# Modulation by quarters and drive chunks begun inside the modulation phase

## What is computed

```python
cond = silu(c)
mod = cond @ w_ada + b_ada                    # 2048 -> 6 * 2048
shift1, scale1, gate1, shift2, scale2, gate2 = split(mod, 6)
h = rms(x, norm1_w) * (1 + scale1) + shift1
proj = h @ w_in                               # 2048 -> 4096
u, q, k, v = split(proj, 4)                   # 1024 columns each
y_ssm = s5_mixer(u, a, dt, b, c, d, w_glu)    # a complex state space model
y_att = dilated_attention(q, k, v)
x = x + gate1 * (concat(y_ssm, y_att) @ w_out)
```

## Time and profile before

| | us |
|---|---|
| median of 3 runs | 3235.0 (3232.37 to 3236.44) |
| the profiled execution | 3236.82 |
| its span | 3234.4 |
| PE busy | 3163.7 (98%) |
| DVE busy | 1813.1 (56%) |
| ACT busy | 1243.5 (38%) |
| POOL busy | 153.2 (5%) |

### The profile page before, as it was taken

The page is one execution under the profiler, slowest core; times in us unless marked ns, Lnnn a source line. Parts: engine busy times, 40 slices in busy tenths (PEclk is TensorE's granted clock), DMA queues, the critical chain, the costliest instruction groups (busy, mean ns, idle before and its releaser), DMA issues.

```text
span 3234.4 us, 56009 instructions
## 1 busy us (share of the span) xinstructions
PE 3163.7 (98%) x24596; PEld 3029.4 (94%) x24596; DVE 1813.1 (56%) x1689; ACT 1243.5 (38%) x1192; POOL 153.2 (5%) x182
## 2 busy tenths in 40 slices
PE   6799999999999999999999999999999999999999
PEld 3599979999999999999999999999999998998997
DVE  0699876775455455654544544555556544454454
ACT  2376633433333333433333333343334333333333
POOL 1534100000000000000000000000030000000000
PEclk7799999999999999999999999999999999999999
DMA  9876667776555555555555555567535555555554
GB/s 346 293 251 235 231 230 247 249 264 222 183 182 182 182 182 182 182 170 179 171 175 175 171 180 170 180 174 152 130 124 186 180 192 180 187 182 190 186 182 156
DMA packets 329090, 631.92 MB, mean 195 GB/s; under 512 B 22452, under 2 KB 24264, under 8 KB 328664
## 3 DMA queue, kind: packets, MB, share of 16 engines
q1 hardware_dynamic: 317896, 626.16, 59.7%
q10 hardware_dynamic: 11040, 3.51, 0.5%
HBM read 627.53 MB, written 2.10 MB: 195 GB/s over the span
## 4 chain that ended last, share of the span: by engine, by line
PE 81%; DVE 3%; issue 1%; ACT 1%; DMA 0%; DVEq 0%; ACTq 0%
PE ps L579 20%; PE ps L580 20%; PE ps L581 20%; PE ps L609 3%; PE ps L611 3%; PE ps L610 3%; PE ps L2037 2%; PE ps L2039 2%; PE ps L2038 2%; DVE w_lo L446 1%; ACT w_hi L441 1%; PE ps L2074 1%; PE ps L2076 1%; PE ps L2075 1%; PE ps L1811 1%
## 5 line engine op out<-in xcount | busy, mean ns | idle before, releaser
L446 DVE TENSOR_TENSOR w_lo<-raw,w_hi 128x2048 fp32r<-128x2048 f32 x496 | 1141.5, 2301 | 1204.6 <-ACT w_hi L441 1204.3
L441 ACT ACTIVATE w_hi<-raw 128x2048 fp32r<-128x2048 f32 x496 | 949.6, 1915 | 1662.5 <-PE ps L581 1273.2
L579 PE MATMUL ps<-act_hi,w_hi 128*128 128x258 f32 (+2 forms) x3328 | 952.9, 286 | 17.1 <-DVE act_lo L676 9.1
L580 PE MATMUL ps<-act_lo,w_hi 128*128 128x258 f32 (+2 forms) x3328 | 952.0, 286 | 0.0
L581 PE MATMUL ps<-act_hi,w_lo 128*128 128x258 f32 (+2 forms) x3328 | 949.6, 285 | 0.0
L579 PE MATMUL ps<-hid_hi,w_hi 128*128 128x256 f32 (+1 forms) x2816 | 796.3, 283 | 0.5 <-DVE w_lo L446 0.5
L580 PE MATMUL ps<-hid_lo,w_hi 128*128 128x256 f32 (+1 forms) x2816 | 795.6, 283 | 0.0
L581 PE MATMUL ps<-hid_hi,w_lo 128*128 128x256 f32 (+1 forms) x2816 | 794.5, 282 | 0.0
L579 PEld LDWEIGHTS ps<-act_hi,w_hi 128*128 128x128 f32 x3328 | 630.6, 189 | 21.6 <-issue 15.9
L580 PEld LDWEIGHTS ps<-act_lo,w_hi 128*128 128x128 f32 x3328 | 630.9, 190 | 0.1
L581 PEld LDWEIGHTS ps<-act_hi,w_lo 128*128 128x128 f32 x3328 | 630.7, 190 | 0.0
(11 more groups left out here) (371 smaller groups left out, 2793.3 us busy)
## 6 DMA issues: line engine op xcount, KB each, us to landing
raw<-in_w_ada SPq DMA_DIRECT2D x96, 1024.0 KB, 5.8
raw<-in_ffn_w_gate SPq DMA_DIRECT2D x88, 1024.0 KB, 5.1
raw<-in_ffn_w_up SPq DMA_DIRECT2D x88, 1024.0 KB, 5.1
raw<-in_ffn_w_down SPq DMA_DIRECT2D x88, 1024.0 KB, 5.1
raw<-in_w_in SPq DMA_DIRECT2D x64, 1024.0 KB, 6.6
raw<-in_w_ffn_gate SPq DMA_DIRECT2D x44, 1024.0 KB, 5.2
raw<-in_w_ffn_up SPq DMA_DIRECT2D x44, 1024.0 KB, 5.2
raw<-in_w_ffn_down SPq DMA_DIRECT2D x44, 1024.0 KB, 5.1
```

The source lines that it names most:

```text
L441: act.activation(w_hi[b][:, :, :], raw[j % RING][:, :, :], ACT.Copy).then_inc(hi_ready, 1)
L446: dve.tensor_tensor(w_lo[b][:, :, :], raw[j % RING][:, :, :], w_hi[b][:, :, :].bitcast(F32), ALU.subtract).then_inc(lo_ready, 1)
L579: pe.matmul(o, whi, hi_, start=(k == 0 and not (shared and m % 2)), stop=False)
L580: pe.matmul(o, whi, lo_, start=False, stop=False)
```

## The change

- `ada1` becomes one phase of 24 V chunks (shift1, and scale1's first two quads), the first four S chunks, four V chunks, two S, four V, two S. So the eight drive chunks are loaded inside it; they now go by quarters of the contraction, both column halves in turn (`first_in`).
- Shift1 is added whole; each quad of scale1 is then summed, turned into `gain` and used for its quarter of the activations (`quarter`, `strip_copy`, `group_sum`). PE does S chunks 0 to 2 after the second quarter, then the strips of the third, chunks 3 and 4, the strips of the fourth, chunks 5 to 7.
- `w_in` keeps 24 S chunks (8 to 31) and all 32 V chunks, in the order S, V, S, V, S, V, V.
- The turns start at chunk 8 instead of 5; so that they end at 31 as before, three chunks (19, 24, 29) have two turns ahead of them. The small sums move to turn 1 or to single turns.
- `c_powers` moves from DVE to POOL, behind `fr` of the next block.
- ACT starts the load of `c_nat` after the norm's root instead of ahead of `params_act`; all squares are summed ahead of the second V group. Several tiles lie elsewhere.

```diff
-    add("ada1", 8, 0, 4, "VVVV")
-    add("w_in", 4, 2, 4, "SV" * 8)
+    add("ada1", 1, 2, 4, "V" * 24 + "SSSS" + "VVVVSS" * 2)
+    add("w_in", 1, 6, 4, "SVSVSVV" * 8)
...
+        def drive_out(act, g):
+            act.wait_ge(chunk_done, 7 + g)
+            src = half_tiles(g)
+            for t in range(4):
+                for j in range(STEP):
+                    ins = act.activation(proj[32 * j:32 * j + 32, 4 * g:4 * g + 4, step_cols(t)],
+                                         src[32 * t:32 * t + 32, :, j:SEQ:STEP], ACT.Copy)
+            ins.then_inc(bank_free[g], 2)
...
-        BASE = 5
+        SLOT_AT = (8, 9, 10, 11, 12, 13, 14, 15, 16, 17, 18, 19, 19, 20, 21, 22, 23, 24, 24, 25, 26, 27, 28, 29, 29, 30, 31)
...
@@ ssm_pool
                 pool.tensor_tensor(fr[:, :, :], fr[:, :, :], kk[:, :, :], ALU.subtract).then_inc(fr_ready, 1)
+                if i:
+                    c_powers(pool, i - 1)
+            c_powers(pool, BLOCKS - 1)
...
@@ ssm_dve
-            if slot == 2 and i < BLOCKS:
-                c_powers(dve, i)
...
-        HEADS_AT = (17, 20, 23, 26)
+        HEADS_AT = (17, 20, 25, 27)
-        GATE1_AT = (5, 8, 14, 17, 20, 26, 29)
+        GATE1_AT = (12, 15, 18, 22, 25, 28, 30)
...
@@ scalar
+                norm_act(act, 0)
+                norm_act(act, 1)
+                for n in range(4):
+                    split_hi(act, ada, 0, at_[n])
+                split_hi(act, ada, 0, at_[4])
+                norm_act(act, 2)
+                split_hi(act, ada, 0, at_[5])
+                split_hi(act, ada, 0, at_[6])
+                norm_act(act, 3)
+                split_hi(act, ada, 0, at_[7])
...
+                    if m in (8, 9):
+                        drive_out(act, m - 8)
...
@@ vector
+                def quarter(q, second):
+                    strip_copy(4 + q)
+                    dve.wait_ge(mod_sum, 5 + q)
+                    four_ = slice(4 * q, 4 * q + 4)
+                    dve.tensor_tensor(gain[:, four_], ps[:, 5, 16 + 4 * q:20 + 4 * q], bada[:, SCALE1 + 4 * q:SCALE1 + 4 * q + 4], ALU.add).then_inc(quad_read, 1)
+                    dve.wait_ge(quad_read, q + 2)
+                    link(dve, "dve", dve.tensor_scalar(gain[:, four_], gain[:, four_], 1.0, None, ALU.add))
+                    link(dve, "dve", dve.tensor_tensor(gain[:, four_], gain[:, four_], vecs[:, V_N1 + 4 * q:V_N1 + 4 * q + 4], ALU.mult))
+                    norm_dve(dve, q, second)
+
+                quarter(0, nothing)
+                quarter(1, nothing)
+                for n in range(4):
+                    split_lo(dve, ada, 0, at_[n])
+                quarter(2, lambda: split_lo(dve, ada, 0, at_[4]))
+                split_lo(dve, ada, 0, at_[5])
+                quarter(3, lambda: split_lo(dve, ada, 0, at_[6]))
+                split_lo(dve, ada, 0, at_[7])
...
@@ tensor
+                for g in range(1, 6):
+                    strips(g)
+                    group_sum(g - 1)
+                    if g == 2:
+                        params_pe(pe)
+                    if g == 4:
+                        c_turns()
+                group_sum(5)
+                pe.wait_ge(c_ready, 1)
+                for n in range(3):
+                    first_in(n)
+                strips(6)
+                group_sum(6)
+                first_in(3)
+                first_in(4)
+                strips(7)
+                group_sum(7)
+                for n in range(5, 8):
+                    first_in(n)
```

More of the change, by code:

```diff
@@ L1344, in ssm_pe, with ssm_pe_turn @@
         def ssm_pe(pe, m):
-            i, slot = ssm_turn(m, 0)
-            if slot == 0 and i == BLOCKS:
+            for i, slot in ssm_turns(m):
+                ssm_pe_turn(pe, m, i, slot)
+        def ssm_pe_turn(pe, m, i, slot):
+            if slot == 1:
                 small_sums(pe, m, i)
@@ L1350, in ssm_pe @@
                 b = i % 2
[L1351 removed]
+                if SLOT_AT[3 * i - 1] != m:
+                    small_sums(pe, m, i)
                 pe.wait_ge(e_pow, 2 * i + 2)
@@ L1543, in _ @@
-                run_phase(dve, "w_in", split_lo, nothing, lambda second: norm_dve(dve, "norm1", gain, 0, 0, second), gate1_acc(dve), norm=True,
-                          peel=4, beside=lambda m: (ssm_dve(dve, m), heads_dve(dve, m)))
+                dve.wait_ge(pre_pool, 6)
+                dve.reciprocal(q_(13), q_(13)).then_inc(inverse, 1)
+                mean_dve(dve, "norm1", 4)
+                root_dve(dve, "norm1")
+                for g in (1, 2, 3):
+                    strip_copy(g)
@@ new lines, in _ @@
+                quarter(0, nothing)
[6 more added lines that the diff above has]
+                split_lo(dve, ada, 0, at_[7])
+                dve.wait_ge(pre_pool, PRE_STEPS)
+                run_phase(dve, "w_in", split_lo, nothing, None, gate1_acc(dve), beside=lambda m: (ssm_dve(dve, m + 8), heads_dve(dve, m + 8)))
@@ new lines, in first_in @@
+                def first_in(n):
+                    c, g = divmod(n, 2)
+                    if c == 0:
+                        pe.wait_ge(res_in, QUADS + 1)
+                    pe.wait_ge(act_ready, ACT0["norm1"] + c + 1)
+                    pe.wait_ge(lo_ready, n + 1)
+                    for t, m in [(t, m) for t in range(CK) for m in range(4)]:
+                        k = CK * c + t
+                        o = out_tile("w_in", g, m, SEQ)
+                        whi, wlo = w_hi[n % 2][:, t, P * m:P * m + P], w_lo[n % 2][:, t, P * m:P * m + P]
+                        hi_, lo_ = act_hi[:, k, SEQ_COLS], act_lo[:, k, SEQ_COLS]
+                        pe.matmul(o, whi, hi_, start=(k == 0 and m % 2 == 0), stop=False)
+                        pe.matmul(o, whi, lo_, start=False, stop=False)
+                        mm = pe.matmul(o, wlo, hi_, start=False, stop=(k == KT - 1 and m % 2 == 1))
+                    mm.then_inc(chunk_done, 1)
@@ L1608, in _ @@
-                products(pe, "w_in", act_hi, act_lo, SEQ_COLS, counted(act_ready, ACT0["norm1"]), beside=lambda m: ssm_pe(pe, m))
+                group_sum(5)
[10 more added lines that the diff above has]
+                    first_in(n)
@@ L1609, in _ @@
+                products(pe, "w_in", act_hi, act_lo, SEQ_COLS, counted(act_ready, ACT0["norm1"]), beside=lambda m: ssm_pe(pe, m + 8))
                 pe.wait_ge(y_ready, BLOCKS)
```

225 lines of the change are left out of this document (108 added, 117 removed).

## The result

The changed kernel is **slower by 9 us**: 3242.1 us (median of 11 runs) against 3233.0 in the same comparison (11 runs), a ratio of 1.0027 with a 95% interval from 1.0019 to 1.0035. The forecast was 3228.4, faster by 6.6.

A forecast was written before the change was run, and what follows sets the result against it. PE set the pace before, with DVE close; after the change DVE would set the end: 181.1 + 209.6 + 2.7 puts the barrier at 393.4, 6.6 us earlier, so 3235.0 - 6.6 = 3228.4 us; 8-in-10 range 3217 to 3243.

The forecast's parts named there:

- The opening: Up to the states' input of block 0 (181.1): first `w_in` matmul at 100.1 instead of 123.57, chunk 6 ending at 159.
- ACT's tables with their load: End of ACT's chain after chunk 6: five short instructions and a table load, estimated at 3.0 us.
- first wait before chunk 11: Sign in the `w_in` phase: PE waits for `w_lo`, first before chunk 11; no size given.
- the doubled turns: Chunks with two turns ahead: POOL's 18 us barely hidden behind PE's 18.5; 5 us each twice if POOL needs 14.
- My landings with strip, copy and sum: Opening, ahead of chunks 3 and 5: lone V chunk lands in 5.3 us, then strip 1.0, copy 0.7, sum 1.0.
- The price of POOL: `w_in` phase: DVE loses about 0.2 us per us of POOL; 72 us more POOL make 14 us (9 to 22).
- full blocking: Rival, 1%: each us of POOL takes one of DVE, 109 us more; 102 us slower, 3337.
- PE by itself: barrier 384: `w_in` phase: PE's own work after `drive_out`, 209 us plus 5, would end at 381, barrier 384; so DVE sets the end.
- The chain at the end: End of the `w_in` phase: last split and the barrier behind it take 2.7 us.
- The sum again, along DVE: DVE from 181.1: 189.9 work, 3.7 gaps, 14 contention, 2 waits, then 2.7: barrier at 393.4 instead of 399.98.
- POOL becomes the bound: Rival, 10%: `c_powers` cost 12 us or more, K waits about 11, DVE loses 25; 15 us slower, 3250.
- DVE does not bind: Rival, 18%: DVE loses under 0.1 us per us of POOL, PE's sum holds; barrier 384, 16 us faster, 3219.

The follow-up runs named there:

- e12: Changed kernel with powers of C of blocks 1 to 7 left out and order VSVSVVS for the first seven buffers: 3225.7 us, ratio 0.9977.
- e2: Changed kernel with the powers of C of blocks 1 to 7 left out: 3231.2 us, ratio 0.9993.
- e4: Changed kernel with V chunks half as wide in the drive's phase (256 of 512 columns): 3228.8 us, ratio 0.9984.
- e7: Changed kernel with POOL computing the four products of the powers of C twice in each block: 3250.4 us, ratio 1.0050.
- e15: Changed kernel with four more one-input POOL instructions in each block, behind the powers of C: 3249.2 us, ratio 1.0054.
- e5: Kernel before the change with only the powers of C moved from DVE to POOL: 3233.4 us, ratio 1.0001.
- e9: On e8, the powers of C of block 0 computed early on POOL, ahead of the norm: 3234.9 us, ratio 1.0006.
- e14: On e9, the edit of e10 plus the third batch of the head's sums at chunk 23 instead of 25: 3234.0 us, ratio 1.0004.
- e10: On e9, two of three steps of the turns' fractions moved from POOL to ACT in blocks 1 to 7: 3232.6 us, ratio 1.0002.
- e8: Changed kernel with order VSVSVVS instead of SVSVSVV for the first seven buffers of the drive's phase: 3236.0 us, ratio 1.0011.

## Why the prediction was wrong, step by step

**The opening held, nearly.** First `w_in` matmul 101.1 (100.1 forecast), chunk 3 at 127.9 (125.5), chunk 5 at 148.4 (143.8), chunk 6 ended at 160.7 (159), states' input of block 0 at 182.9 (181.1). ACT's tables with their load, the 3.0 that no row had shown, took 2.9 (179.9 to 182.8). DVE above 95% busy in the phase, PE under it, first wait before chunk 11, POOL at 142 (some 135), no wait worth naming on the doubled turns (0.2 us): as written. My landings with strip, copy and sum add up to 8.0 us each in two places where I wrote 8.4, which changes nothing.

**The price of POOL was mis-sized.** I took 0.2 us per us from one pair of V chunks and splits and got 14 us; the runs give 0.29 to 0.32 and 23 us. This term of the sum is the first step that failed. The pair ran beside E's steps, where 3.98 for 3.11 is 28% more and 2.69 for 2.28 is 18%. In after's trace a V instruction takes 765 ns beside `kk`, 902 beside the products of E, 1029 beside the products of C, and 1098 beside the sums into `cp`: what was to be added was the dearest kind, and what I measured was a mixture. The upper bound of that term (22) would have been nearly right. On the Trainium skill's page "SBUF — State Buffer", section "Who interferes with whom", a DVE instruction with two SBUF inputs contends with a GpSimd instruction that reads SBUF. The trace agrees as to the pair (two inputs on DVE) and shows a grade the sentence lacks, 0.04 us per us for one input on POOL and 0.3 for two. Of the full blocking that the prediction quotes the V chunks show nothing: beside the dearest kind they took 1098 ns for 751, 1.46 times. The page "GPSIMD Engine Reference", section "2.1 Instruction dispatch", says that POOL's two inputs take turns on one read port, which would fit; no run here shows the port.

**"PE by itself: barrier 384" was wrong by the coupling,** the second step that failed. The sum of PE's own work was fair: e12, with DVE nearly out of the way, has 387.2. But I let PE run through while DVE was behind. The gap is local: from the start of chunk 8 to the start of chunk 11 PE has only 20.2 us of work (three chunks, E, S; 168.9 to 189.1), and DVE has three splits, four V chunks and the states' input, 7.2 + 15.7 + 4.7 = 27.6 us. That is 7.4 more. DVE also stood idle for 5.9 us in it, mostly waiting for ACT's `w_hi` behind the drive's copies, and had begun 3.9 us ahead of PE: 7.4 + 5.9 - 3.9 = 9.4, the wait. I saw the two V chunks in a row and listed the wait as a sign, but gave it no price. It costs 9.3 us of PE, and the chunk behind it takes 7.2 instead of 5.9 us, its first part at half clock. It could cost nothing only if DVE alone set the end, and it didn't: e2 and e4 freed DVE of 20 us or more and got 10.9 and 13.3, with this wait still there (9.3 and 7.1).

**The chain at the end** took 6.0 us from the last V chunk to the barrier, not 2.7, since PE's last chunk ended 2.3 us behind the V chunk and the last split stood behind it.

The sum again, along DVE: 393.4 forecast, +1.8 (start), +9 (contention), +3.3 (end), less 1.5 as a remainder that no row explains, is 406. Along PE, from chunk 8 on: it is idle for 13.2 us up to its last chunk, before for 1.8, and loses some 4 us more to the lower clock (an estimate from the stretches at 0.5 that are not idle: 22 us against 14, half of each). That is 15 of the 16 us between a lead of 10 and a lag of 6.

**The rivals.** "POOL becomes the bound" (10%) was the one on the right side, yet not by its mechanism: `c_powers` took 8.4 us in block 0 and about 10 later, and K waited 0.2 us. It gave DVE's loss as 25, near the 23 that came. e7 and e15 show its point of decision: 35 to 55 us more of POOL and K waits 4 to 11 us. "DVE does not bind" is refuted by e4. Full blocking at its price of 109 us is refuted by every run. The range (3217 to 3243) held the time, at its edge. The chance of 0.12 for slower was too small, as I judge it now: contention at its own upper bound would have put the barrier at 401, with the wait before chunk 11 on top, and the two together are no rare case.

**Where the expected gain went**, then: 10 us of lead at 169; PE gives 9.3 back at once before chunk 11, because eight S chunks were moved ahead without the eight V chunks that used to stand between them (2 of 32 are done at 182, instead of 8), and some 8 more through DVE instructions lengthened by POOL's two-input work (the barriers of e2 and after, 398.0 and 406.1; 10.9 by the medians). Their sum, 17, is a little over the 16 us; how the two overlap is not shown. What the powers' move saves DVE it loses again (e5).

## What to carry to other kernels

Moving work from one engine to a neighbour that shares something with it has a price on the work that stays: measure it for the very form that will be added (here two inputs, 0.3 us per us beside V chunks and nearly 0.5 beside the norm's short instructions), and take no average over other forms. When chunks of one kind are moved ahead, the other kind stays behind as a debt: sum each engine's work between two neighbouring due times, not over the phase, since a local surplus of 7 us on one engine became, with its own waits, 9 us of idle time on the other, which no later slack gave back. And place free-standing work (V chunks) into idle stretches that come before the crowded one: one changed string gave two thirds of the loss back.

## What the runs showed of the hardware

- A 128x512 instruction of DVE with two inputs in SBUF takes 751 ns alone, 765 to 783 beside a one-input `tensor_scalar` of POOL, 902 beside its 128x192 products, and 1029 to 1098 beside its two-input products of 128x256 and sums of 64x256. A 128x2048 split takes 2284 ns alone, 2365 beside `kk` (e15) and 2818 beside the sums.
- A 128x272 instruction of DVE (four in the norm) takes 0.50 us alone, 0.87 beside POOL's 128x256 products (e9), and 0.96 to 1.04 beside its 64x256 sums (e14).
- DVE's 128x4 `tensor_scalar` with one input (`gain`) took 0.17 us in five of the kernels built on after. In after and seven others a MEMSET of POOL was under way, and it took 0.33 to 1.75 us and ended within 0.03 us of the end of a MEMSET (e10: DVE 87.26 to 89.01, MEMSET 87.19 to 88.99). This is part of the spread of the start.
- POOL's own instructions are uneven: the 64x256 sums took 1.05 to 1.2 us as a rule beside DVE, and now and then 2.6 to 2.8.
- PE's granted clock fell to its lower level (0.5) in the 9.3 us wait of after, from 191.1 to 201.3, so that wait costs more than its length. It also fell without any wait: from 263.0 to 266.4 in before, behind 3.6 us of small matmuls (sums and E from 259.4), and at 272.8 in e12 during K. A chunk that met the lower level took up to 8.7 us (348.8 to 357.5 in after) instead of 5.9, and K 4.05 (e8) instead of 2.19.
